# Parking the residual in DRAM during a mixture-of-experts stage, with half of one expert's up weights in its place

## The chip, the cores and the metric

The kernel runs on one core of one Trainium2 chip. The metric is device time in microseconds (us) of one execution; smaller is better.

## What is computed

One decoder layer for 256 prompt tokens and 8 sample tokens, 264 in all, in float32 with a model width of 1024. The part around the change is the second half:

```python
x = x + gate_m * jnp.einsum('ntd,de->nte', merged, lw['w_out'])
h2 = rmsnorm(x, lw['g_norm_ffn']) * (1.0 + scale_f) + shift_f
x = x + gate_f * moe_ffn(h2, lw)
...
a = jnp.einsum('td,edf->tef', hb, lw['w_e_gate'])
b = jnp.einsum('td,edf->tef', hb, lw['w_e_up'])
routed = jnp.einsum('tef,efd->td', jax.nn.silu(a) * b * gates[..., None], lw['w_e_down'])
```

There are 64 experts of inner width 256. Each has 2 MB of gate and up weights (called *up weights* here; 1 MB for each half of the 1024 input rows) and 1 MB of down weights. Each token goes to 8 experts. A shared expert is added to all tokens.

## The kernel before

Activations lie with features on the 128 partitions: `xT` is the residual (128 x 8 x 264), `hT` the normalised tokens. The first half of the program (attention, convolution and gate mixers, output projection) ends with the residual after the mixers in `xT`; each of its 8 tiles adds one to the semaphore `x1`. The same step makes `xa`, the scaled input of the second norm. After that `xT` is not read until the end of the program, when the sum of the experts is scaled and added to it (`scaled`, 16 VectorE operations) and it is stored as output.

**The handover to the experts.** The normalised tokens are transposed to rows (`h2tok`) and stored to a DRAM table `h2rows` together with the gates `lg`, from which GpSimd gathers each expert's tokens by indirect DMA. `hT` itself is stored to `h2kept` (read again only in a fallback for overfull experts), because its place then takes weights.

**The expert stage** goes over 32 pairs of experts (`pair(p)`, experts 2p and 2p+1). For each pair TensorE does the up product of the two halves (`up`: 32 matmuls of 64 x 512 into bank pA, 16 for each half of the input rows), spreads the result of the pair before to its tokens (`spread_samples`, `spread`), transposes the activations (`act_tr`), and does the down product (`down`, banks pB and pC). GpSimd gathers the tokens of pair q into `xs` (`gather`), three pairs ahead of their use in the steady state; VectorE computes the indices (`index`), the gates' column (`gate_column`) and the activation.

**The order of the transfers** is written by hand in SyncE's program: one queue, in which each transfer waits for its semaphores and all behind it wait too. `refill(p)` reloads the ring for pair p + 2: each half of the up weights after pair p has released it (semaphore `gu`), the down weights after `dn`. A 2 MB transfer brings one half of the up weights of both experts (16 KB a partition). Parts of three experts (KEPT = 19, DOWN = 37, AGAIN = 43) are loaded early into tensors that have become free, and left out of the refills (`alone`).

GpSimd issues the gathers on a queue of its own. Before the first gather it waits for the stores of the gates (`d_tok`) and rows (`d_rows2`), and for `idx`. SyncE waits for the first gather (`d_x[0]`) before it overwrites `hT`. These are the lines of the handover that set the order:

```python
pool.wait_ge(d_tok, 16 * 2)
pool.wait_ge(d_rows2, 16 * 3)
...
sp.wait_ge(d_x[0], 16)
sp.dma_start(hTf[:, 0:1024], expert_up(KEPT, 1, 2, 4).rearrange("p k c -> p (k c)")).then_inc(d_kept, 16)
```

The first is at line 823, the last two at 677 and 678.

Of the kernel before, what the change touches and what calls it, by code (L numbers as in the profile page):

```python
# [9 lines left out]
F32 = mybir.dt.float32  # L10
# [4 lines left out]
P = 128  # L15
D = 1024
DT = D // P
NP_ = 256
NS = 8
NT = NP_ + NS  # L20
# [10 lines left out]
E = 64  # L31
# [68 lines left out]
MID = KEPT // 2  # L100
DOWN = 2 * MID + 19
AGAIN = DOWN + 6


PLACE = (0, 3, 2, 1)
# [3 lines left out]
HALF_K = DT // 2  # L109
# [3 lines left out]
def place(e):  # L113

    return ORDER[(e - 1) % NSLOT]
# [92 lines left out]
def build(nc, A, O):  # L208

    with ExitStack() as ctx:  # L210
# [8 lines left out]
        xT = sb("xT", [P, DT, NT])  # L219
# [51 lines left out]
        lg = sb("lg", [P, 3, E])  # L271
# [42 lines left out]
        xa = pT[:].rearrange("p t n -> p (t n)")[:, 0:DT * NB].rearrange("p (k c) -> p k c", k=DT)  # L314
        free_p = pT[:].rearrange("p t n -> p (t n)")[:, DT * NB:NTILE * NT]
        shifts = ksq[:, 1, 0:3 * NC].rearrange("p (x c) -> p x c", x=3)
        h2tok = [xs[:, 0, 0:D], xs[:, 1, 0:D], qTf[:, 0:D]]
# [25 lines left out]
        sact = qTf[:, D:D + FT * NT].rearrange("p (f t) -> p f t", f=FT)  # L343
        sactg = [abuf[:, 512:512 + NT], rstd[:]]
        zpf = zp[:].rearrange("p k t -> p (k t)")
        first_gu = [adx[:, k, :] for k in range(CT)] + [kTf[:, k * 512:(k + 1) * 512] for k in range(CT)]
        hTf, h2f = hT[:].rearrange("p k t -> p (k t)"), free_p[:, 0:3 * D]
        wrf, bsf = wrou[:].rearrange("p k e -> p (k e)"), bsp[:].rearrange("p k t -> p (k t)")
# [17 lines left out]
        def up_part(b):  # L366
            return part(b, GU_AT[b], DT, 2 * FE)
# [3 lines left out]
        def up_halves(b):  # L371
            pair_at = ringf[:, PAIR_AT[b]:PAIR_AT[b] + 4 * DT * FE]
            return pair_at.rearrange("p (h x c) -> p h x c", h=2, x=2)[:, :, SECOND[b]]

        def up_rows(b):
            at = [PAIR_AT[b] + (2 * (k // HALF_K) + SECOND[b]) * HALF_K * 2 * FE + k % HALF_K * 2 * FE for k in range(DT)]
            return [ringf[:, x:x + 2 * FE] for x in at]
# [41 lines left out]
        d_in = sem("small_inputs")  # L419
# [7 lines left out]
        d_first = sem("first_expert")  # L427
# [19 lines left out]
        d_tok = sem("gates_stored")  # L447
        d_rows2 = sem("h2_stored")
        d_x = [sem("tokens_gathered0"), sem("tokens_gathered1")]
        c_f = sem("vector_chain_dense")  # L450
        norms = nc.dram_tensor("head_norms", (2, H, NT), F32, kind="Internal").ap()
        h2kept = nc.dram_tensor("h2_kept", (P, DT, NT), F32, kind="Internal").ap()
        h2rows = nc.dram_tensor("h2_rows", (NT, D + E), F32, kind="Internal").ap()

# [8 lines left out]
        def _(sp):  # L463
# [143 lines left out]
            def expert_down(e):  # L607
                return A["w_e_dn"][e // 2][:, 1 - e % 2]
# [20 lines left out]
            def two(w, p):  # L629
                return A[w][p] if isinstance(p, int) else A[w][bass.ds(p, 1)].rearrange(  # L630
                    "o p h x k c -> (o p) h x k c" if w == "w_e_gu" else "o p x k c -> (o p) x k c")
# [4 lines left out]
            def down_load(b, p, x, to):  # L636
                sp.dma_start(down_part(b), two("w_e_dn", p)[:, 1 - x]).then_inc(wgd[to], 16)
# [4 lines left out]
            def half_load(q, h, b):  # L642
# [12 lines left out]
            reuse(3, "exp")  # L655
            half_load(1, 1, 3)
            down_load(3, 0, 1, 3)
            n = BASE["rout"]
            sp.wait_ge(full[n % 4], n // 4 + 1)
            sp.dma_start(wrf, expert_down(KEPT)[:, 1, 0:512]).then_inc(d_kept, 16)  # L660
            sp.wait_ge(s["h2s"], 1)
            sp.wait_ge(s["h2"], DT)
            sp.dma_start(h2kept, hT[:]).then_inc(d_kept, 16)
# [1 line left out]
            sp.wait_ge(full[n % 4], n // 4 + 1)  # L665
            sp.dma_start(pT[:].rearrange("p t n -> p (t n)")[:, 0:FT * D], expert_down(0).rearrange("p f c -> p (f c)")
                         ).then_inc(d_first, 16)
            for j, m in enumerate((P, P, NS)):
                sp.wait_ge(s["h2tok"], 2 * j + 2)
                sp.dma_start(h2rows[j * P:j * P + m, 0:D], h2tok[j][0:m]).then_inc(d_rows2, 16)  # L670
            sp.wait_ge(s["mask_gates"], 2)
            sp.dma_start(h2rows[0:NP_, D:D + E].rearrange("(j p) e -> p j e", p=P), lg[:, 0:2, :]).then_inc(d_tok, 16)
            sp.dma_start(h2rows[NP_:NT, D:D + E], lg[0:NS, 2, :]).then_inc(d_tok, 16)
            sp.wait_ge(d_kept, 16 * 7)
            n = BASE["shup1"]
            sp.wait_ge(full[n % 4], n // 4 + 1)
# [9 lines left out]
            def refill(p, i):  # L686
                q = p + 2
                at = q if i is None else i * 2 + q
                alone = i is None and 2 * q + 1 in (KEPT, AGAIN)
                for h, (b, _) in enumerate((ups(q), second_ups(q))):  # L690
                    n = 2 * p + 1 + h
                    sp.wait_ge(s["gu"], n if i is None else i * 4 + n)
                    if alone:
                        sp.dma_start(up_halves(0)[:, h], two("w_e_gu", at)[:, h, 0].rearrange("p k c -> p (k c)")
                                     ).then_inc(wgt[b], 16)
                    else:
                        sp.dma_start(up_pair[q % 2 == 1][:, h], two("w_e_gu", at)[:, h].rearrange("p x k c -> p (x k c)")
                                     ).then_inc(wgt[b], 16)
                sp.wait_ge(s["dn"], 2 * p + 2 if i is None else i * 4 + (2 * p + 2))
                if q % 2:  # L700
                    down_load(0, at, 0, 0)
                    if i is not None or 2 * q + 1 not in (KEPT, AGAIN):
                        down_load(1, at, 1, 1)
                elif i is None and 2 * q + 1 == DOWN:
                    down_load(2, at, 0, 2)
                else:
                    sp.dma_start(down_pair, two("w_e_dn", at).rearrange("p x k c -> p (x k c)")).then_inc(wgd[2], 16)

            for h in range(2):
                sp.wait_ge(s["gu"], h + 1)  # L710
                sp.dma_start(up_part(1).rearrange("p (h k) c -> p h (k c)", h=2)[:, h], expert_up(4 + h, 1).rearrange("p k c -> p (k c)")
                             ).then_inc(wgt[1], 16)
                sp.dma_start([adx[:].rearrange("p k c -> p (k c)"), kTf[:, 0:CT * 512]][h],
                             expert_up(AGAIN, h).rearrange("p k c -> p (k c)")).then_inc(d_first, 16)
# [16 lines left out]
            with sp.Fori(0, (NPAIR - 14 - MID - 1) // 2) as i:  # L731
                for p in (MID + 12, MID + 13):
                    refill(p, i)
            refill(NPAIR - 3, None)

            sp.wait_ge(s["flag"], 1)
            over = sp.value_load(flag[0:1, 0:1], min_val=0, max_val=1)
# [111 lines left out]
        def _(pe):  # L849
# [82 lines left out]
            for m in range(6):  # L932
                n = BASE["in0"] + m
                t = enter(n)
# [40 lines left out]
            for h in range(H):  # L975
                n = BASE["q"] + h
                t = enter(n)
# [10 lines left out]
            for h2 in range(H // 2):  # L988
                n = BASE["k"] + h2
                t = enter(n)  # L990
# [6 lines left out]
            for b in range(2):  # L997
                n = BASE["v"] + b
                t = enter(n)
# [45 lines left out]
            t = enter(n)  # L1045
# [5 lines left out]
            t = enter(n)  # L1051
            for hf in range(2):
                for j in range(4):
                    h = 4 * hf + j
# [3 lines left out]
            m = BASE["qlatT"]  # L1058
            t = enter(m)
# [155 lines left out]
            for c in range(CT):  # L1215
                n = BASE["uvs"] + c
                t = enter(n)
# [62 lines left out]
            t = enter(n)  # L1280
# [117 lines left out]
            def up(p, i):  # L1398
                if p:
                    pe.wait_ge(s["xt"], turn(i, p + 1, 1))  # L1400
                else:
                    pe.wait_ge(s["h2x"], DT + 1)
                if 2 <= p < NPAIR - 2:
                    pe.wait_ge(s["idx"], turn(i, p + 3, 1))
                gu = []
                for e in (2 * p, 2 * p + 1):
                    if e == 0:
                        pe.wait_ge(d_first, 16 * 5)
                        gu.append(first_gu)
                    elif e == KEPT:  # L1410
                        pe.wait_ge(d_kept, 16 * 11)
                        gu.append(kept_gu)
                    elif e == AGAIN and i is None:
                        pe.wait_ge(d_first, 16 * 9)
                        gu.append(first_gu)
                    else:
                        if e == 1:
                            pe.wait_ge(wgt[1], arrival(1, "exp"))
                        elif e % 2 == 0:
                            b, n = ups(p)  # L1420
                            pe.wait_ge(wgt[b], turn(i, n, 8))
                        gu.append(up_rows(place(e)) if p else [up_part(place(e))[:, k, :] for k in range(DT)])
                for k in range(DT):
                    if k == HALF_K and p == 0:
                        pe.wait_ge(s["xt"], 1)
                    if k == HALF_K and p:
                        b, n = second_ups(p)
                        pe.wait_ge(wgt[b], turn(i, n, 8))
                    for x in range(2):
                        last = mm(pA[CAP * x:CAP * (x + 1), :], xTs[:, p % 2, k, CAP * x:CAP * (x + 1)], gu[x][k],  # L1430
                                  k == 0, k == DT - 1)
                    if k == HALF_K - 1:
                        last.then_inc(s["gu"], 1)
                last.then_inc(s["gu"], 1)
# [506 lines left out]
        def _(dve):  # L1941
# [624 lines left out]
            V.tensor_copy(gm_last, gm[(NPAIR - 1) % 4][:, 0:NT])  # L2566
            for p in range(29, NPAIR):
                pair(p)
            for m in range(DT):
                if m % 4 == 0:  # L2570
                    dve.wait_ge(s["spread"], 2 + m // 4)
                scaled(m, acc[m]).then_inc(s["sums"], 1)
# [168 lines left out]
```

## Time and profile before

| | us |
|---|---|
| median of 3 runs | 971.5 |
| lowest and highest run | 970.04, 972.77 |
| the profiled execution, its own time | 971.65 |
| span of the profiled execution | 969.8 |
| PE busy | 940.4 (97%) |
| DVE busy | 561.1 (58%) |
| ACT busy | 201.9 (21%) |
| DMA, mean over the span | 322 GB/s |

Granted TensorE clock: 0.997 over the span. Busy PE contains matmuls that are in flight and wait for their weights' turn, so 97% doesn't say that PE sets the time. Which engine does so differs from stage to stage; it is read from who waits for whom in a stretch, and from the rate of the DMA engines there. In the rows below, a time in the first column is us from the span's start, SPq is SyncE's queue of issued transfers, L860 is the helper that issues every matmul, and `oaT`, `qT`, `vtok` and `sinT` are tensors whose space the expert stage uses again (its activations, its transposed tokens, the pair's result, and small tables). `h_rows` is `h2rows`, `h_kept` is `h2kept`.

### The profile page before, as it was taken

What the parts mean: (1) busy time and instruction counts of PE and PEld (TensorE: products, weight loads), DVE (VectorE), ACT (ScalarE), POOL (GpSimd) and SP (SyncE); (2) the same over time, 40 slices, a digit from 0 to 9 for tenths busy, and PEclk for the clock granted to TensorE, in tenths of its full rate; (3) what the DMA queues carried; (4) which work ended last, traced back from release to release, by engine and by line L of the source; (5) the groups of instructions that cost most, each with busy time, mean ns of one, the idle gap of its engine ahead of it and who ended that gap; (6) DMA issues with size and microseconds to landing.
All of it is one profiled execution on the core that took longest, in us unless ns stands there. A gap on an engine that the chain in (4) does not pass through costs nothing.

```text
span 969.8 us, 15335 instructions
## 1 busy us (share of the span) xinstructions
PE 940.4 (97%) x5400; PEld 537.9 (55%) x5401; DVE 561.1 (58%) x1389; ACT 201.9 (21%) x416; POOL 56.3 (6%) x77
## 2 busy tenths in 40 slices
PE   6999999999999999999999999999999999999997
PEld 2488867544446788888644444444444344434343
DVE  2613322367864010123738877888888788886864
ACT  3321241335435200002511111111111111111111
POOL 0000010100000000000011000000100000000000
PEclk9999999999999999999999999999999999999999
DMA  8995559756546295537679999999999999999994
GB/s 304 419 416 237 183 193 324 229 155 171 169 136 271 99 384 222 217 130 282 263 299 424 424 425 424 396 423 423 429 424 425 423 424 422 426 427 423 422 428 156
DMA packets 54228, 312.03 MB, mean 322 GB/s; under 512 B 9018, under 2 KB 28506, under 8 KB 33426
## 3 DMA queue, kind: packets, MB, share of 16 engines
q1 hardware_dynamic: 47986, 298.10, 77.4%
q0 software_dynamic: 5904, 12.79, 3.7%
q8 instruction: 42, 0.69, 0.3%
q10 hardware_dynamic: 272, 0.26, 0.1%
q14 instruction: 24, 0.20, 0.1%
HBM read 315.80 MB, written 3.95 MB: 330 GB/s over the span
## 4 chain that ended last, share of the span: by engine, by line
PE 72%; DMA 19%; SPq 4%; DVE 2%; issue 2%; ACT 0%; DVEq 0%; POOLq 0%
PE bank L860 45%; PE pA L860 17%; DMA ring<-in_w_e_gu 16%; PE pB L860 4%; PE pC L860 4%; SPq L493 2%; PE pD L860 1%; DMA ring<-in_w_bg 1%; SPq L537 1%; DMA pT<-in_poolT 1%; PE pA L1439 0%; DMA xs<-h_rows,idx 0%; DVE rstd L1963 0%; DVE xT L2506 0%; SPq L532 0%
## 5 line engine op out<-in xcount | busy, mean ns | idle before, releaser
L860 PE MATMUL pA<-ring,qT 128*64 128x512 f32 x976 | 227.6, 594 | 9.2 <-DMA ring<-in_w_e_gu 9.2
L2489 DVE STREAM_TRANSPOSE qT<-xs 32x256 f32<-32x256 f32 x480 | 209.2, 436 | 7.7
L860 PE MATMUL bank<-hT,ring 128*128 128x264 f32 (+1 forms) x832 | 189.4, 388 | 0.9 <-DMA ring<-in_w_bg 0.9
L860 PEld LDWEIGHTS bank<-hT,ring 128*128 128x128 f32 (+1 forms) x832 | 154.3, 189 | 31.6 <-issue 4.7
L860 PEld LDWEIGHTS pA<-ring,qT 128*64 128x64 f32 x976 | 72.8, 137 | 154.0 <-issue 137.9
L860 PE MATMUL bank<-wuk,ring 128*128 128x512 f32 x192 | 87.0, 601 | 0.0
L860 PE MATMUL bank<-pT 128*128 128x256 bf16 (+1 forms) x499 | 85.4, 273 | 0.2 <-issue 0.2
L860 PE MATMUL bank<-pT,vtok 128*128 128x256 bf16 (+1 forms) x264 | 71.8, 281 | 0.0
L860 PE MATMUL pB<-ring,oaT 128*64 128x512 f32 x240 | 62.0, 605 | 0.0
L860 PE MATMUL pC<-ring,oaT 128*64 128x512 f32 x240 | 60.4, 592 | 0.0
L832 POOL DMA_INDIRECT xs<-h_rows,idx x32 | 36.0, 1125 | 407.1 <-DVE idx L2466 306.6
L860 PEld LDWEIGHTS bank<-wuk,ring 128*128 128x128 f32 x192 | 35.4, 192 | 41.9 <-issue 40.6
L2527 DVE SCALAR_TENSOR_TENSOR oaT<-oaT,sinT,pA 128x256 f32<-128x256 f32 x32 | 15.4, 480 | 74.3 <-ACT oaT L1902 74.3
L1902 ACT ACTIVATE oaT<-pA 128x256 f32<-128x256 f32 x32 | 12.3, 384 | 215.1 <-PE pA L860 215.1
L860 PEld LDWEIGHTS bank<-pT 128*128 128x128 bf16 x500 | 48.9, 98 | 6.3 <-issue 0.8
L2499 DVE TENSOR_TENSOR pT<-vtok 128x512 f32<-128x512 f32 x62 | 41.8, 686 | 12.2 <-ACT vtok L1912 10.0
L860 PE MATMUL bank<-pT,ring 128*128 128x264 f32 (+1 forms) x208 | 48.6, 388 | 0.0
L2082 DVE TENSOR_REDUCE xs<-ksq 128x8 f32<-128x512 f32 x48 | 32.3, 685 | 21.1 <-ACT ksq L1725 19.3
L860 PEld LDWEIGHTS bank<-pT,ring 128*128 128x128 f32 x208 | 39.3, 190 | 7.3 <-issue 0.4
L2503 DVE TENSOR_TENSOR pT<-pT 128x512 f32<-128x512 f32 x62 | 39.9, 684 | 0.0
L1912 ACT ACTIVATE vtok<-pB 128x512 f32<-128x512 f32 x32 | 19.1, 597 | 99.4 <-PE pB L860 99.4
L860 PEld LDWEIGHTS pC<-ring,oaT 128*64 128x64 f32 x240 | 18.4, 137 | 35.3 <-issue 35.3
(380 smaller groups left out, 914.6 us busy)
## 6 DMA issues: line engine op xcount, KB each, us to landing
ring<-in_w_e_gu SPq DMA_DIRECT2D x58, 2048.0 KB, 19.7
ring<-in_w_e_dn SPq DMA_DIRECT2D x34, 1024.0 KB, 16.2
ring<-in_w_e_dn SPq DMA_DIRECT2D x13, 2048.0 KB, 17.5
ring<-in_poolT SPq DMA_DIRECT2D x64, 208.0 KB, 2.8
ring<-in_w_ada SPq DMA_DIRECT2D x12, 1024.0 KB, 10.4
ring<-in_w_bg SPq DMA_DIRECT2D x4, 3072.0 KB, 11.0
ring<-in_w_mix SPq DMA_DIRECT2D x5, 2048.0 KB, 9.8
ring<-in_w_ada SPq DMA_DIRECT2D x4, 2048.0 KB, 12.9
```

The source lines that it names most:

```text
L493: return sp.value_load(ptab[0:1, bass.ds(x, 1)], min_val=0, max_val=NPOOL - 1)
L537: sp.dma_start(rowpg[g][x], A["poolR"][bass.ds(page(g * HALF + x), 1)] .rearrange("o r c -> (o r) c")).then_inc(d_rows, 16)
L832: nc.gpsimd.indirect_dma_start(out=xs[:, q % 2, :], out_offset=None, in_=h2rows, in_offset=bass.IndirectOffsetOnAxis(ap=idx[:, q % 2:q % 2 ...
L860: return nc.tensor.matmul(out, lhsT, rhs, start=start, stop=stop)
L1902: nc.scalar.activation(silu_s, pA[:, 0:FE], ACT.Silu).then_inc(s["silu_s"], 1)
L1912: nc.scalar.activation(yrow[:, hf * 512:(hf + 1) * 512], t[:], ACT.Copy).then_inc(s["y"], 1)
L2082: V.tensor_reduce(out=kss[:, q, j, :], in_=ksq[:, j % 2, :].rearrange("p (h d) -> p h d", h=H), op=ALU.add, axis=AX.X).then_inc(s["ksq_use ...
L2489: last = V.transpose(xTs[32 * j:32 * j + 32, q % 2, :, 32 * a:32 * a + 32], src[32 * a:32 * a + 32, j])
L2499: V.tensor_tensor(rest_y[:, c], yrow[:, c], parts_y[0][:, c], ALU.subtract).then_inc(s["rest"], 1)
L2503: V.tensor_tensor(low_y[:, c], rest_y[:, c], parts_y[1][:, c], ALU.subtract).then_inc(s["low"], 1)
L2527: V.scalar_tensor_tensor(out=act_s, in0=silu_s, scalar=gcol[:, p % 2:p % 2 + 1], in1=pA[:, FE:2 * FE], op0=ALU.mult, op1=ALU.mult).then_in ...
```

## The change

The residual is written to a new DRAM tensor `x1kept` as soon as its 8 tiles are there, and read back into `xT` by a transfer behind the last weights; VectorE waits for that before the final scaling. In between, `xT` holds the first half of the up weights of expert AHEAD = 41, and the refill of that half (pair 20, in `refill(18)`) brings only expert 40's: 1 MB where it was 2. In the handover the stores of token rows and gates stand ahead of the store of `hT` and of the load of expert 0's down weights. A wait for that load (`d_first`) is added ahead of the later loads that use its semaphore.

```diff
+AHEAD = AGAIN - 2
...
+        x1kept = nc.dram_tensor("x1_kept", (P, DT, NT), F32, kind="Internal").ap()
...
             half_load(1, 1, 3)
             down_load(3, 0, 1, 3)
+            sp.wait_ge(s["x1"], DT)
+            sp.dma_start(x1kept, xT[:]).then_inc(d_in, 16)
...
             sp.dma_start(wrf, expert_down(KEPT)[:, 1, 0:512]).then_inc(d_kept, 16)
+            for j, m in enumerate((P, P, NS)):
+                sp.wait_ge(s["h2tok"], 2 * j + 2)
+                sp.dma_start(h2rows[j * P:j * P + m, 0:D], h2tok[j][0:m]).then_inc(d_rows2, 16)
+            sp.wait_ge(s["mask_gates"], 2)
+            sp.dma_start(h2rows[0:NP_, D:D + E].rearrange("(j p) e -> p j e", p=P), lg[:, 0:2, :]).then_inc(d_tok, 16)
+            sp.dma_start(h2rows[NP_:NT, D:D + E], lg[0:NS, 2, :]).then_inc(d_tok, 16)
             sp.wait_ge(s["h2s"], 1)
             sp.wait_ge(s["h2"], DT)
             sp.dma_start(h2kept, hT[:]).then_inc(d_kept, 16)
...
-            for j, m in enumerate((P, P, NS)):
-                sp.wait_ge(s["h2tok"], 2 * j + 2)
-                sp.dma_start(h2rows[j * P:j * P + m, 0:D], h2tok[j][0:m]).then_inc(d_rows2, 16)
-            sp.wait_ge(s["mask_gates"], 2)
-            sp.dma_start(h2rows[0:NP_, D:D + E].rearrange("(j p) e -> p j e", p=P), lg[:, 0:2, :]).then_inc(d_tok, 16)
-            sp.dma_start(h2rows[NP_:NT, D:D + E], lg[0:NS, 2, :]).then_inc(d_tok, 16)
+            sp.wait_ge(d_in, 16 * 3)
+            sp.wait_ge(s["sq2"], DT)
+            sp.wait_ge(s["xa"], DT)
+            sp.dma_start(xTf[:, 0:2048], expert_up(AHEAD, 0).rearrange("p k c -> p (k c)")).then_inc(d_in, 16)
...
-                    if alone:
-                        sp.dma_start(up_halves(0)[:, h], two("w_e_gu", at)[:, h, 0].rearrange("p k c -> p (k c)")
+                    if alone or i is None and h == 0 and 2 * q + 1 == AHEAD:
+                        sp.dma_start(up_halves(0 if q % 2 else 2)[:, h], two("w_e_gu", at)[:, h, 0].rearrange("p k c -> p (k c)")
...
+            sp.wait_ge(d_first, 16 * 6)
...
             refill(NPAIR - 3, None)
+            sp.wait_ge(d_in, 16 * 4)
+            sp.dma_start(xT[:], x1kept).then_inc(d_in, 16)
...
+                        if e == AHEAD and i is None:
+                            pe.wait_ge(d_in, 16 * 4)
+                            gu[-1] = [xTf[:, k * 512:(k + 1) * 512] for k in range(HALF_K)] + gu[-1][HALF_K:]
...
             for p in range(29, NPAIR):
                 pair(p)
+            dve.wait_ge(d_in, 16 * 5)
```

SyncE's queue in the handover, before (`wrou` takes a part of KEPT's down weights, `pT` expert 0's down weights, `hT`, `ksq` and `abuf` parts of KEPT and DOWN):

```order
L637 DMA ring<-in_w_e_dn 128x2048
L660 DMA wrou<-in_w_e_dn 128x512
L663 DMA h_kept<-hT 128x2112
L666 DMA pT<-in_w_e_dn 128x2048
L670 DMA h_rows<-xs 128x1024 x2
L670 DMA h_rows<-qT 8x1024
L672 DMA h_rows<-lg 128x2x64
L673 DMA h_rows<-lg 8x64
L678 DMA hT<-in_w_e_gu 128x1024
L679 DMA hT<-in_w_e_dn 128x1024
```

And of the change (`x_kept` is `x1kept`):

```order
L640 DMA ring<-in_w_e_dn 128x2048
L662 DMA x_kept<-xT 128x2112
L665 DMA wrou<-in_w_e_dn 128x512
L668 DMA h_rows<-xs 128x1024 x2
L668 DMA h_rows<-qT 8x1024
L670 DMA h_rows<-lg 128x2x64
L671 DMA h_rows<-lg 8x64
L674 DMA h_kept<-hT 128x2112
L677 DMA pT<-in_w_e_dn 128x2048
L682 DMA xT<-in_w_e_gu 128x2048
L687 DMA hT<-in_w_e_gu 128x1024
L688 DMA hT<-in_w_e_dn 128x1024
```

The five stores of rows and gates have moved past two transfers of 1 MB, a store of the residual stands ahead of them, and three transfers of 1 MB now stand between them and the loads into `hT`.

SyncE's queue at the refills of pairs 20 to 22, of the change; before, the first of these rows and the second were one, of 128x4096 x2:

```order
L703 DMA ring<-in_w_e_gu 128x2048
L706 DMA ring<-in_w_e_gu 128x4096
L716 DMA ring<-in_w_e_dn 128x4096
L703 DMA ring<-in_w_e_gu 128x2048 x2
L640 DMA ring<-in_w_e_dn 128x2048
```

One transfer has half its width; nothing else has moved there.

## Rows read from the trace of the kernel before

**Rows 1.** GB/s of the DMA engines in 40 slices of the span, from the page.

```profile
GB/s 304 419 416 237 183 193 324 229 155 171 169 136 271 99 384 222 217 130 282 263 299 424 424 425 424 396 423 423 429 424 425 423 424 422 426 427 423 422 428 156
```

**Rows 2.** Waits in 494:732 (first row, TensorE's longest), then in 732:970.

```profile
PE pB L860 <- ACT oaT L1909: 0.7, 1, 0.7
...
PE pA L860 <- DMA ring<-in_w_e_gu: 9.2, 11, 1.3
```

**Rows 3.** Windows: us, PE, PEld, DVE, ACT, POOL busy, clock, DMA share, GB/s.

```profile
475.00:480.00 5.00, 5.00 (x29) 4.18 (x28) 4.53 (x46) 1.19 (x3) 0.00 (x0) 1.00 0.74 262
...
486.00:490.00 4.00, 4.00 (x21) 3.32 (x20) 2.87 (x14) 0.39 (x1) 1.49 (x2) 1.00 0.03 5
...
512.00:612.00 100.00, 100.00 (x633) 46.78 (x631) 79.80 (x199) 13.13 (x27) 6.97 (x7) 1.00 1.01 424
628.00:636.00 8.00, 8.00 (x55) 3.13 (x51) 5.78 (x14) 0.62 (x2) 0.57 (x1) 1.00 0.94 362
636.00:956.00 320.00, 310.76 (x1920) 135.96 (x1918) 252.59 (x619) 43.53 (x89) 21.65 (x20) 1.00 1.00 419
```

**Rows 4.** The chain of waits from the stores to the first expert: start, us, what.

```profile
483.85 2.86 DMA h_rows<-lg
...
488.00 4.07 DMA xs<-h_rows,idx
...
492.11 0.67 PE pB L1395 x4
```

**Rows 5.** Timeline: first row stores, index, last shared matmuls, second gather, pair 0.

```profile
480.24 1.30 SPq L670 DMA_DIRECT2D h_rows<-xs  x2
...
486.04 0.15 DVE L2466 TENSOR_SCALAR idx<-idxf 128x1 uint32<-128x1 f32 x1
...
488.65 3.06 PE L860 MATMUL bank<-hT,ring 128*128 128x264 f32 x13
...
489.76 0.99 POOL L832 DMA_INDIRECT xs<-h_rows,idx  x1 [0.51 <-issue]
...
493.95 0.60 SPq L643 DMA_DIRECT2D ring<-in_w_e_gu  x1
...
501.36 0.48 DVE L2527 SCALAR_TENSOR_TENSOR oaT<-oaT,sinT,pA 128x256 f32<-128x256 f32 x1 [5.76 <-ACT oaT L1902]
```

**Rows 6.** Transfers issued near 488, 489.8, 495.8 and 612.5: KB, us to landing.

```profile
xs<-h_rows,idx POOLq DMA_INDIRECT x1, 4.1
...
xs<-h_rows,idx POOLq DMA_INDIRECT x1, 3.5
...
xs<-h_rows,idx POOLq DMA_INDIRECT x1, 10.4
...
ring<-in_w_e_dn SPq DMA_DIRECT2D x1, 1024.0 KB, 6.8
xs<-h_rows,idx POOLq DMA_INDIRECT x1, 7.2
```

**Rows 7.** Transfers issued near 465.9, 475.4, 782.3, 493.9: KB, us to landing.

```profile
ring<-in_w_e_dn SPq DMA_DIRECT2D x1, 1024.0 KB, 10.5
...
h_kept<-hT SPq DMA_DIRECT2D x1, 1056.0 KB, 4.2
...
ring<-in_w_e_dn SPq DMA_DIRECT2D x1, 1024.0 KB, 17.2
...
ring<-in_w_e_gu SPq DMA_DIRECT2D x1, 2048.0 KB, 11.7
```

**Rows 8.** The end: chain, then the last two down loads, issued at 930.60.

```profile
923.61 26.58 DMA ring<-in_w_e_gu
...
950.23 3.65 PE pA L860 x16
...
961.86 0.48 DVE xT L2506
...
ring<-in_w_e_dn SPq DMA_DIRECT2D x2, 1024.0 KB, 23.1
```

More of the change, by code:

```diff
@@ L345, in build @@
         zpf = zp[:].rearrange("p k t -> p (k t)")
+        xTf = xT[:].rearrange("p k t -> p (k t)")
         first_gu = [adx[:, k, :] for k in range(CT)] + [kTf[:, k * 512:(k + 1) * 512] for k in range(CT)]
```

## The prediction

> **What bounds the kernel now.** I read the rate by slices first. From slice 21 (about 509 us) to slice 38 the DMA engines move 422 to 429 GB/s, but for one slice of 396 [rows 1]: the expert stage streams at a constant rate. Then who waits: between 494 and 732 us TensorE waits for no weights, its longest wait being 0.7 us for ScalarE; from 732 to the end its matmuls wait 9.2 us, in 11 waits, for up weights [rows 2]. So TensorE sets the pace at first, and from 732 us on the stream does. The chain at the end agrees: the last half of up weights lands at 950.2, and only then come the last 3.65 us of up matmuls [rows 8].
>
> What ties the two together is the last moment at which the stream had nothing to do. That is in 628:636, at 362 GB/s [rows 3]: 8 us x (424 - 362) / 424 = 1.2 us idle, because the refills of pair 9 are small and TensorE had not yet released the next slot. After it the stream has no gap (419 GB/s in 636:956, [rows 3]). So the end is: the time at which TensorE reaches that release, plus all bytes issued later over the rate. A byte less after 636 us shortens the kernel; whatever makes TensorE start the experts later by X lengthens it by X.
>
> That start is the handover. The chain there [rows 4]: the last gates' store is issued at 483.85 and lands 2.86 us later (486.71), GpSimd starts 1.3 us later, and the gather takes 4.07 us from 488.00 and lands at 492.07, TensorE goes on at 492.11. It had its last shared matmuls until 488.65 + 3.06 = 491.71 [rows 5], so it waited 0.4 us. The DMA engines stand nearly idle in 486:490, at 5 GB/s [rows 3].
>
> **The change part by part.**
>
> *Half of an expert less in the stream.* 1024 KB is 1.049 MB; at 424 GB/s [rows 3] that is 2.47 us. It is taken out of a refill issued near 757 us, when the stream is behind, so all of it counts if no new gap opens. The shortest time to landing in the expert stage after that is 17.2 us, for 1 MB issued near 782 [rows 7], a transfer that needs 2.5 us itself: some 12 us of queue are in front of it, and taking 2.5 away leaves it full. And TensorE must be able to use it: it has waited 9.2 us in this part [rows 2]. **-2.5 us.**
>
> *Store of the residual* (1056 KB). It is issued at about 466.7, behind 3 MB of loads of which the last lands at 465.9 + 10.5 = 476.4 [rows 7]. Its own 2.5 us then move the small load behind it and fill part of 475:480, which runs at 262 GB/s with room for 5 x 162 / 424 = 1.9 us [rows 3]. The store lands near 479, before the token rows are ready (their first store goes at 480.24, [rows 5]), and before SyncE's new wait for it. **0**; at worst, if it reaches into the rows' stores, +0.5.
>
> *Reading it back.* It is issued behind the last down loads. These land at 930.6 + 23.1 = 953.7 in the median of the two, about 955 for the second; the residual's 2.5 us end near 957.5, and VectorE's first scaling is at 961.86 [rows 8]. **0**, hidden by some 4 us; without that cover, what it is late.
>
> *New waits.* SyncE comes to those for `x1`, `sq2`, `xa` and the stored residual after their events, and to the one for the sixth `d_first` transfer (expert 0's down load) behind the first gather's landing, when that load is in. **0.** The store of `hT` and that down load are now issued behind the row stores, from 484.6. The first is needed by the load into `hT`, which waits for the gather anyway; the second by pair 0's down product, which comes after the activation at 501.36 [rows 5]. **0**; if either landed late, what it is late.
>
> *Stores of rows and gates first.* They are now issued as soon as VectorE and ScalarE have made the data, and still will be: moving them saves no issue time, only the transfer of expert 0's down weights in front of them. The last store took 2.86 us to land. It can gain at most what lies behind the index: `idx` is ready at 486.04 + 0.15 = 486.19 [rows 5], the stores land at 486.71, so 0.5 us. **-0.5 us** on the gather's start (0 to -0.5), which would be about 487.5. In quiet it would then land at 491.6, and TensorE, free at 491.7, would gain 0.4.
>
> *But the gather is no longer in quiet.* Behind the stores SyncE now issues `hT`'s store (1056 KB), expert 0's down weights (1024 KB) and the half expert (1024 KB), from about 484.6. Counting 1.7 us from issue to first byte (the `hT` store took 4.2 us to land, of which 2.5 are its bytes, [rows 7]), they occupy the engines from 486.3 to 493.8. The gather's own data moves from about 489.6. Now the gather has those 4 us to itself. What company costs it: in quiet 4.1 and 3.5 us; 7.2 beside one load of 1024 KB (rows of 8 KB, as here); 10.4 beside a load of 2048 KB (rows of 16 KB) [rows 6]. The 7.2 landed just after that load (6.8, issued within 0.3 us of it), and the 10.4 (495.8 + 10.4 = 506.2) just after the 2 MB load issued at 493.95, which took 11.7 [rows 5, 7]. So a gather shares each engine row by row with loads and needs about as long as its 8 rows' worth of them. The bounds: 0 (the gather isn't held up), and 4.2 us, the end of the backlog (493.8 - 489.6). The nearest row gives 7.2 - 3.8 = 3.4; one load of eight 8 KB rows an engine is worth 2.5. I take 2.5, since part of the 3.4 was another load of 16 KB rows in front. The gather then lands at 494.1 instead of 492.07: **+2.0 us** (-0.4 to +3.6) on TensorE's start, with nothing to absorb it.
>
> Sum against the profiled execution: 971.65 - 2.5 + 2.0 = 971.2; the median of the runs is 0.15 lower: **971.0 us**, -0.5 us. A measurement of this kernel can tell about 0.3% (2.9 us) from no change.
>
> On the sharing of an engine, the Trainium skill ("DMA: Bandwidth & Descriptors", section on queues, rings and completion order) has a rule: each DMA engine takes turns between queues by whole packets of some 9 to 17 descriptors, not row by row. By that rule the gather would wait only for the load in progress, and the sum would be lower, as rival 2 works out. The trace doesn't quite agree: the 7.2 us gather landed 0.4 us after a whole load issued behind it.
>
> **The rivals.**
>
> 1. *The gather isn't delayed.* For it: a gather has 128 slots and on average 264 x 8 / 32 = 66 tokens, so there is little to move, and GpSimd's queue is another one. Against: of the gathers in [rows 6], none beside a load took less than 7.2. Then TensorE starts 0.4 us earlier: 971.5 - 2.5 - 0.4 = **968.6**.
>
> 2. *It waits only for the transfer in progress.* At 489.6 that is expert 0's down load, whose data ends at about 486.3 + 5.0 = 491.3: 1.7 us of delay, landing at 493.3, X = +1.2: **970.2**.
>
> 3. *It waits for the whole backlog.* X = +3.6: 971.5 - 2.5 + 3.6 = **972.6**, slower, but by less than can be told.
>
> 4. *Slower than before: the second gather takes over the path.* It is issued at 489.76 [rows 5] on the same queue, behind the first, and VectorE waits for it (`gate_column(1)`) ahead of pair 0's activation, which runs at 501.36 [rows 5]. Before, it took 3.5 us and was early by 8. If its rows are not served before the 2 MB load that SyncE issues after the first gather lands (now 493.95, landing at 505.6, [rows 5, 7]), it lands with that load: 4.3 us after the activation needs it, and with rival 3's X the sum is 971.5 - 2.5 + 3.6 + 4.3 = **976.9**. It decides from the point at which the second gather lands later than about 503. Against: between the backlog's end and that load stand four small loads of 1.5 MB, room enough to get through.
>
> 5. *The change doesn't do what it says*: nothing is gained if TensorE, not the stream, sets the last third. The time would be 971.5 + 2.0 = 973.5. But it waited 9.2 us for weights there [rows 2], more than three times what is taken away: excluded.
>
> **How the numbers follow.** Forecast 0.50; rival 1 0.20; rival 2 0.12; rival 3 0.10; rival 4 0.06; anything else 0.02. The likeliest case gives 971.0. The range takes in rival 1 below and rival 3 above, with 0.3 for the measurement: 968.3 to 973.0; rival 4 is left out. Rival 1 lies right at the bound of 0.3%: half of it, and a little for a second gain that I don't see, make faster 0.15; rival 4 and the rest make slower 0.07; same 0.78.
>
> **What the profile would show.** The refill of pair 20 with one row of 1024 KB; from then on, landings 2.5 us earlier relative to TensorE's first expert matmul. The first gather issued at about 487.5 and landing 6 to 7 us later, with the DMA engines over 400 GB/s in 487:494. TensorE waiting some 2.4 us for `xs` before its transposes, where it waited 0.4. The idle 1.2 us of the stream still there, moved by X. The residual's read landed before VectorE asks. I am wrong if the first gather lands within 5 us of its issue, or if the last up weights don't land X - 2.5 us from where they did, or if VectorE waits for the second gather.

## The result, and the profile after

| | before | changed |
|---|---|---|
| median of 16 runs each | 971.54 us | 974.10 us |
| ratio, 95% interval | | 1.0025 (1.0017 to 1.0033) |
| the profiled execution, span | 969.8 us | 971.7 us |

The kernel became 2.6 us slower. That is under the 0.3% that I called the bound, but clear of the noise, on the other side than the forecast of -0.5, and outside the range (968.3 to 973.0). One execution of the changed kernel took 5593 us; it is in the median and not in the ratio.

The two profiled executions differ before the handover already: the index is ready at 486.04 in one and at 484.49 in the other, though nothing ahead of it is known to cost more or less. Two profiles of one and the same kernel (load behind gather, below) differ as much: they have it at 484.42 and 487.37. So the handover is measured from the start of the index computation, not from zero. The chain of waits of the changed kernel there, in the columns start, us and what, beside [rows 4, 5]:

```profile
484.49 0.16 DVE idx L2481
...
484.88 1.13 issue
486.01 7.76 DMA xs<-h_rows,idx
...
493.81 0.67 PE pB L1407 x4
...
495.56 8.35 PE pA L872 x32
```

The gather takes 7.76 us where it took 4.07. From the index to the first expert matmul it was 493.74 - 486.04 = 7.70 us; it is 495.56 - 484.49 = 11.07, so **+3.4**. Then comes what I had not in the sum: pair 0's up product, 32 matmuls, takes 8.35 us, where the same chain before has 7.02 us for it, **+1.3**. Windows of the changed kernel (columns as in [rows 3]) show why:

```profile
486.00:490.00 4.00, 4.00 (x20) 3.13 (x18) 2.01 (x9) 0.39 (x1) 2.24 (x2) 1.00 0.98 394
490.00:494.00 4.00, 0.35 (x3) 0.19 (x3) 0.99 (x3) 0.00 (x0) 0.38 (x1) 1.00 0.70 280
494.00:496.00 2.00, 1.75 (x11) 1.06 (x12) 0.62 (x2) 1.08 (x2) 0.00 (x0) 0.70 0.51 115
496.00:498.00 2.00, 2.00 (x6) 0.47 (x4) 1.33 (x8) 0.00 (x0) 0.37 (x1) 0.50 0.99 394
498.00:500.00 2.00, 2.00 (x12) 0.74 (x10) 0.00 (x0) 0.00 (x0) 0.65 (x1) 0.95 1.15 420
```

The DMA engines, idle in 486:490 before, now move 394 GB/s. TensorE, with nothing to do from 490.2 to 493.8, is granted half its clock (0.50, that is 1.2 GHz instead of 2.4) in 496:498, and three pairs of matmuls take 0.86 us a step instead of 0.43. The clock fell only after the wait: it is 1.00 in 494.0:494.5, where the transposes run, and 0.50 from 495.0 on. The last two transfers that stand in SyncE's queue ahead of the gather, by their own landings (KB, us from issue to landing):

```profile
pT<-in_w_e_dn SPq DMA_DIRECT2D x1, 1024.0 KB, 7.1
xT<-in_w_e_gu SPq DMA_DIRECT2D x1, 1024.0 KB, 10.3
```

The first, issued at 482.71, lands at 489.8, the second, issued at 483.25, at 493.6, and the gather at 493.77: 0.2 us after the last byte that was queued ahead of it.

At the end, chain, then VectorE's timeline, then TensorE's waits in 732:970 of the changed kernel:

```profile
925.49 26.58 DMA ring<-in_w_e_gu
...
952.11 3.65 PE pA L872 x16
```

```profile
959.48 3.23 DVE L2521 SCALAR_TENSOR_TENSOR xT<-bank,ada,xT 128x256 f32<-128x256 f32 x8 [2.71 <-DMA xT<-x_kept]
...
963.74 0.48 DVE L2521 SCALAR_TENSOR_TENSOR xT<-bank,ada,xT 128x256 f32<-128x256 f32 x1 [0.90 <-PE bank L872]
```

```profile
PE pA L872 <- DMA ring<-in_w_e_gu: 8.2, 10, 1.2
```

The end is still the stream's [rows 8]. From the end of pair 0's up product (500.76 before, 503.91 now) to the last up weights it takes 448.2 us, where it took 449.5: 1.3 less, of the 2.5 expected. TensorE's waits for up weights in 732:970 are 8.2 us where they were 9.2 [rows 2]. The ten profiles of kernels that load the half expert, this one among them, gain between 0.6 and 2.5 us in this stretch, the three of kernels without it (below) between -0.2 and +0.15; what sets the size within that spread is not shown. The residual's read lands late enough to hold VectorE 2.7 us, but the wait is covered: from the last up weights to VectorE's ninth scaling it is 11.63 us before and after.

### The profile page after: what moved, and what is told of

It reads as the page before. It is cut to its first block, busy times and chain, and to the rows that moved or that the text cites. A ratio compares the mean times of both kernels' runs of the same rounds, so it can differ in the third digit from the quotient of the medians.

```text
span 971.7 us, 15342 instructions
## 1 busy us (share of the span) xinstructions
PE 940.5 (97%) x5400; PEld 538.4 (55%) x5401; DVE 561.4 (58%) x1389; ACT 201.8 (21%) x416; POOL 56.3 (6%) x77
## 4 chain that ended last, share of the span: by engine, by line
PE 73%; DMA 17%; SPq 6%; issue 2%; DVE 2%; ACT 0%; DVEq 0%; POOLq 0%
PE bank L872 44%; PE pA L872 18%; DMA ring<-in_w_e_gu 13%; PE pB L872 5%; PE pC L872 4%; SPq L496 3%; PE pD L872 1%; SPq L540 1%; DMA ring<-in_w_bg 1%; SPq L535 1%; DMA pT<-in_poolT 1%; DMA xs<-h_rows,idx 1%; PE pA L1454 0%; DVE xT L2521 0%; DMA ring<-in_poolT 0%
## 5 line engine op out<-in xcount | busy, mean ns | idle before, releaser
L872 PE MATMUL bank<-wuk,pT 128*128 128x512 f32 x64 | 30.9, 634 | 7.7 <-DMA pT<-in_poolT 7.7
```

Of the source, the lines that this page charges most:

```text
L872: return nc.tensor.matmul(out, lhsT, rhs, start=start, stop=stop)
```

## The experiments

Each is a short edit of one of the two kernels; the kernel before ran beside them. "Handover" is the time from the index to the first expert matmul, less the 7.70 us of before, plus the up product of pair 0 less 7.02, both from one profiled execution each. "Time" is the median less that of the kernel before on the same chip. The kernels are named by what they do; "rows first" means that the rows and gates are stored ahead of `hT`.

| kernel | residual parked | half expert's load | rows first | handover, us | time, us | ratio, 95% |
|---|---|---|---|---|---|---|
| changed | yes | ahead of gather | yes | 3.4 + 1.3 | +2.6 | 1.0017 to 1.0033 |
| order alone | no | none | yes | 0.1 + 0 | -0.2 | 0.9985 to 1.0010 |
| parking, old order | yes | none | no | 3.0 + 0.5 | +3.7 | 1.0027 to 1.0048 |
| parking, new order | yes | none | yes | -0.1 + 0 | -1.2 | 0.9983 to 1.0004 |
| all, old order | yes | ahead of gather | no | 2.5 + 1.5 | +1.0 | 0.9997 to 1.0024 |
| load behind gather | yes | behind it | yes | 0.1 + 0 | **-2.1** | 0.9966 to 0.9989 |
| the same again | | | | 0.1 + 0 | **-1.8** | 0.9974 to 0.9993 |
| store behind gates | yes, later | behind it | no | 0.4 + 0 | -1.4 | 0.9972 to 0.9994 |
| load ahead of rows | yes | first | yes | 1.9 + 0 | +0.6 | 1.0001 to 1.0023 |
| load behind landing | yes | ahead, held | no | 3.4 + 1.7 | +3.3 | 1.0013 to 1.0034 |
| warm | as changed | | | 4.2 + 0 | +1.2 | 0.9995 to 1.0024 |
| one more store | as changed | | | 5.8 + 2.0 | +5.5 (one run) | |
| two more stores | as changed | | | 5.8 + 0.5 | +6.6 (one run) | |

**All, old order.** The changed kernel with the stores of the rows and gates back behind `hT`'s store and expert 0's down load, ahead of the half expert's load.

```diff
-            for j, m in enumerate((P, P, NS)):
-                sp.wait_ge(s["h2tok"], 2 * j + 2)
-                sp.dma_start(h2rows[j * P:j * P + m, 0:D], h2tok[j][0:m]).then_inc(d_rows2, 16)
-            sp.wait_ge(s["mask_gates"], 2)
...
-            sp.dma_start(h2rows[NP_:NT, D:D + E], lg[0:NS, 2, :]).then_inc(d_tok, 16)
...
+            for j, m in enumerate((P, P, NS)):
+                sp.wait_ge(s["h2tok"], 2 * j + 2)
+                sp.dma_start(h2rows[j * P:j * P + m, 0:D], h2tok[j][0:m]).then_inc(d_rows2, 16)
+            sp.wait_ge(s["mask_gates"], 2)
...
+            sp.dma_start(h2rows[NP_:NT, D:D + E], lg[0:NS, 2, :]).then_inc(d_tok, 16)
```

> The changed kernel with the old order of the stores: hT's store and expert 0's down load ahead of the rows and gates, and the half expert's load directly behind the gates. Theory A (the change loses only in the handover: the first gather lands with the last transfer queued ahead of it, and TensorE, having waited, starts at half its clock): now only 1 MB is queued behind the gates and its data is through before the gather's own begins, so the gather takes 4 to 5 us again, TensorE waits under 1 us, its clock stays at 1.0, and the 2.5 us in the stream are kept: 1.5 to 2.5 us faster than the kernel before, about 969.3. Rival B (parking the residual itself costs: its store, its reading back, or the added waits): still as slow as the changed kernel, ratio 1.001 to 1.003 to the kernel before. Rival C (the 2.5 us of the stream are not there to be had): time equal to the kernel before.

Not faster: +1.0 us. The gates themselves are late in it:

```profile
483.48 5.58 DMA h_rows<-lg
...
490.35 4.17 DMA xs<-h_rows,idx
...
496.31 8.53 PE pA L872 x32
```

The gather is quiet again (4.17 us), as theory A had it, but the last store of the gates takes 5.6 us to land instead of 2.9 [rows 4], TensorE waits 2.8 us, and the clock falls. So something ahead of the gates or behind them is new, and this kernel cannot say which.

**Order alone.** The kernel before, with the same six lines moved the other way: ahead of `hT`'s store and expert 0's down load, and the wait for `d_first` that goes with it. Nothing is parked and no load added.

```diff
+            for j, m in enumerate((P, P, NS)):
+                sp.wait_ge(s["h2tok"], 2 * j + 2)
+                sp.dma_start(h2rows[j * P:j * P + m, 0:D], h2tok[j][0:m]).then_inc(d_rows2, 16)
+            sp.wait_ge(s["mask_gates"], 2)
...
+            sp.dma_start(h2rows[NP_:NT, D:D + E], lg[0:NS, 2, :]).then_inc(d_tok, 16)
...
-            for j, m in enumerate((P, P, NS)):
...
-            sp.dma_start(h2rows[NP_:NT, D:D + E], lg[0:NS, 2, :]).then_inc(d_tok, 16)
```

> The kernel before with the new order alone: rows and gates stored ahead of hT's store and expert 0's down load, no parking and no half expert. Theory A: 2 MB are now queued between the gates and the gather and end some 2 to 2.5 us sooner than the 3 MB of the changed kernel; the gather takes 5.5 to 6.5 us, TensorE waits 1 to 2 us, and with nothing won in the stream the time is 0.5 to 3 us above the kernel before, the more if the wait is long enough to halve the clock. If the new order itself were a gain (gates 0.5 us sooner), the time would be 0.4 us below.

```profile
486.58 4.58 DMA xs<-h_rows,idx
...
pT<-in_w_e_dn SPq DMA_DIRECT2D x1, 1024.0 KB, 7.0
```

Neither loss nor gain. With 2 MB behind the gates the gather takes 4.6 us, half a microsecond more than in quiet, given back by the gates' earlier landing. The expected 5.5 to 6.5 us was wrong. The second of the two transfers, issued at 483.28, is not through when the gather is issued; it lands at 490.3, 0.9 us ahead of it. One transfer still in progress, with nothing behind it, costs half a microsecond. It is the third megabyte, queued behind that one, that does the harm.

**Load behind gather.** The changed kernel, with the half expert's load and its waits moved behind the last load ahead of the refills.

```diff
-            sp.dma_start(xTf[:, 0:2048], expert_up(AHEAD, 0).rearrange("p k c -> p (k c)")).then_inc(d_in, 16)
...
             half_load(2, 0, 2)
+            sp.dma_start(xTf[:, 0:2048], expert_up(AHEAD, 0).rearrange("p k c -> p (k c)")).then_inc(d_in, 16)
```

> The changed kernel with the half expert's load moved behind the wait for the gather (behind the first 2 MB load of pair 2). Theory A: the gather meets the same 2 MB as in the order-alone kernel and takes 5.5 to 6.5 us; the stream gets 1 MB more early, where it has 1.2 to 1.7 us of slack before pair 9, and 1 MB less later: about 1 us gained, so 0 to 2 us above the kernel before, and under the changed kernel by 1 to 2 us. Rival B (parking costs): no better than the changed kernel.

```profile
485.94 4.59 DMA xs<-h_rows,idx
...
492.21 7.02 PE pA L872 x32
```

-2.1 us, better than expected, and better than both kernels. From the end of pair 0's up product to the last up weights it takes 2.1 us less than before. The early stream takes the megabyte into the gap that it had: the window 628:636, which ran at 362 GB/s [rows 3], is now nearly full.

```profile
628.00:636.00 8.00, 8.00 (x61) 4.10 (x58) 6.02 (x16) 0.77 (x2) 0.00 (x0) 1.00 0.99 414
```

**Warm.** The changed kernel, with sixteen matmuls that compute nothing used, ahead of the wait for the gather.

```diff
             shared_up("shup1", FE + P, range(DT))
+            pe.wait_ge(s["h2tok"], 6)
+            for _ in range(16):
+                mm(pC[:, 0:P], ones[:], ones[:], True, True)
             tokens_tr(0)
```

> The changed kernel with 16 matmuls of 128x128 on ones (3.4 us of work whose result isn't used) in TensorE's program where it waits for the gather. Theory A's second half: the granted clock stays at 1.0, pair 0's up product takes 7.0 us instead of 8.4, and the time is 1.3 us below the changed kernel, about +0.9 us to the kernel before. Rival: the slow first matmuls come from something else (DMA traffic on the weights' memory, the transposed tokens late), and the time stays at the changed kernel's, +2.4 us.

The gather takes 8.7 us, and yet pair 0 runs at full clock: windows of this kernel, the granted clock third from the end.

```profile
494.00:496.00 2.00, 0.98 (x9) 0.79 (x8) 0.42 (x2) 0.00 (x0) 0.00 (x0) 1.00 0.05 13
496.00:498.00 2.00, 1.75 (x12) 0.82 (x12) 0.77 (x2) 1.08 (x2) 0.00 (x0) 1.00 0.66 176
```

The up product is back at 7.02 us with the same queue, so the 1.3 us were the clock's and not the traffic's. The time is at +1.2, 1.4 under the changed kernel's, near the 1.3 expected, but the two intervals overlap, and the 1.4 is not the clock alone: in the profiles this kernel's handover is 0.8 us longer before the first matmul, and from the end of the up product to the last up weights it takes 951.14 - 504.17 = 447.0 us, 2.5 less than before, where the changed kernel took 1.3 less.

**One more store.** The changed kernel, with `hT` stored once more, to a place that nobody reads. SyncE waits for that store before it loads over `hT`, so the time of this kernel and of the one with two holds more than the gather's delay.

```diff
             sp.dma_start(xTf[:, 0:2048], expert_up(AHEAD, 0).rearrange("p k c -> p (k c)")).then_inc(d_in, 16)
+            sp.dma_start(h2more, hT[:]).then_inc(d_in, 16)
```

> The changed kernel with one more store of hT (1056 KB, to a tensor that nothing reads) behind the half expert's load and ahead of the gather. Theory A (a gather lands only when everything queued ahead of it is through): the gather takes about 2.5 us longer than in the changed kernel, 10 to 11 us. Rival (the gather takes turns row by row with the load it meets, so it is through with its eight rows' worth of company): it stays at 7.8 to 8.7 us.

The gather takes 9.7 us, between the two theories; two more stores, below, tell them apart.

**Parking, old order.** The kernel before, with the residual stored, its place left empty and read back late, and the waits of the change.

```diff
+            sp.wait_ge(s["x1"], DT)
+            sp.dma_start(x1kept, xT[:]).then_inc(d_in, 16)
...
+            sp.dma_start(xT[:], x1kept).then_inc(d_in, 16)
...
+            dve.wait_ge(d_in, 16 * 4)
```

> The kernel before with the parking alone: the residual stored and read back, nothing loaded in its place, stores in the old order, all refills whole. Theory A: no cost, within 0.5 us of the kernel before. Rival B (parking costs): 1 us or more above it.

+3.7 us, where theory A had no cost. The chain, then the landings of `hT`'s store and of expert 0's down load:

```profile
482.74 5.72 DMA h_rows<-lg
...
489.75 4.14 DMA xs<-h_rows,idx
...
493.94 1.11 PE pB L1404 x4
```

```profile
h_kept<-hT SPq DMA_DIRECT2D x1, 1056.0 KB, 7.2
...
pT<-in_w_e_dn SPq DMA_DIRECT2D x1, 1024.0 KB, 7.3
```

Before, they landed in 4.2 us [rows 7] and 4.9. The residual's store, 1 MB earlier in the same queue, pushes each transfer behind it back by 2.4 to 3 us, down to the gates, which land in 5.7 us instead of 2.9. TensorE waits 2.9 us (491.05 to 493.94), and here the clock is at 0.50 before it resumes: its transposes take 1.11 us instead of 0.67. This also explains the all-old-order kernel, whose gates took 5.6.

**Load ahead of rows.** The changed kernel, with the half expert's load and its waits moved up, behind KEPT's small load.

```diff
             sp.dma_start(wrf, expert_down(KEPT)[:, 1, 0:512]).then_inc(d_kept, 16)
+            sp.dma_start(xTf[:, 0:2048], expert_up(AHEAD, 0).rearrange("p k c -> p (k c)")).then_inc(d_in, 16)
...
-            sp.dma_start(xTf[:, 0:2048], expert_up(AHEAD, 0).rearrange("p k c -> p (k c)")).then_inc(d_in, 16)
```

> The changed kernel with the half expert's load ahead of the rows' stores, as soon as the residual's store has landed, where the DMA engines stand idle for some 2 us. Its bytes are through some 2.5 us before the gather's begin, but the rows and gates are now stored behind it. If small stores land late only because of what is queued AHEAD of them: gates land about 1 us later than the index is ready, the gather takes 4.6 us as in the order-alone kernel, and the time is 1 to 2.5 us below the kernel before. If, as the run with the old order suggests, the gates' stores are also held up by the loads queued BEHIND them (there the last store, 2 KB, took 5.6 us against 2.9), they now land only with hT's store or expert 0's down load, 2 to 3 us after the index, and the time is 0 to 2 us above the kernel before.

+0.6 us, in the second branch. The gather starts 487.82 - 484.70 = 3.1 us after the index began, where order alone has 1.5, and takes 4.8 us. What stands ahead of the rows' stores is enough to explain it; whether loads behind small stores delay them too, these kernels don't separate.

**Load behind landing.** The all-old-order kernel, where the half expert's load waits until the rows and gates have landed.

```diff
+            sp.wait_ge(d_tok, 16 * 2)
+            sp.wait_ge(d_rows2, 16 * 3)
             sp.dma_start(xTf[:, 0:2048], expert_up(AHEAD, 0).rearrange("p k c -> p (k c)")).then_inc(d_in, 16)
```

> The old order of stores with the half expert's load held until the rows' and gates' stores have landed. If in the old-order run the load held up the stores queued in front of it, the stores now land in 2.9 us and the gather starts as in the kernel before, 1.8 us after the index. Its data then meets one load of 1 MB with 1 to 1.5 us still to go: 4.5 to 6 us instead of 4.1. TensorE waits 1 to 2 us; time 0.5 to 2 us below the kernel before, against +1.0 for the old-order run.

```profile
484.12 6.00 DMA h_rows<-lg
...
491.42 4.80 DMA xs<-h_rows,idx
```

Missed: +3.3 us. Its gates take 6.0 us with nothing behind them, so the load behind was not to blame. The load then starts only at 490.1 and meets the gather, which takes 4.8 us beside it and lands 0.6 us after it.

**Store behind gates.** The load-behind-gather kernel, with the stores of the rows and gates in the old order and the residual's store behind them.

```diff
-            sp.dma_start(x1kept, xT[:]).then_inc(d_in, 16)
             sp.dma_start(wrf, expert_down(KEPT)[:, 1, 0:512]).then_inc(d_kept, 16)
...
             sp.dma_start(h2rows[NP_:NT, D:D + E], lg[0:NS, 2, :]).then_inc(d_tok, 16)
+            sp.dma_start(x1kept, xT[:]).then_inc(d_in, 16)
```

> Old order of the stores, with the residual's store moved behind the gates' and the half expert's load behind the gather. If the parking cost 3.7 us only because its store stood ahead of hT's and pushed everything up to the gates back, that is gone: the gates' last store lands in about 2.9 us again, the store's own bytes go through the idle 486 to 489 us, the gather takes 4 to 5 us, and the time is that of the kernel with the load behind the gather, 1.5 to 2.5 us below the kernel before. If the parking costs in another place (the end, the early stream), it stays 1 us or more above.

```profile
484.23 3.25 DMA h_rows<-lg
...
488.78 4.16 DMA xs<-h_rows,idx
```

-1.4 us, just short of the 1.5 to 2.5 expected. The parking's cost is gone without the new order, by putting its store into the idle stretch. The gather takes 4.2 us although the window 486:490 is busy to 301 GB/s, for the store is through (landing at 490.0) when its rows come.

**Two more stores.** The kernel with one more store, with a second one behind it.

```diff
+            sp.dma_start(h2most, hT[:]).then_inc(d_in, 16)
```

> The kernel with one more store of hT, and a second one behind it: 5.3 MB queued between the gates and the gather instead of 4.3 and 3.2. If a gather had to wait for all that is queued ahead of it, 2.5 us more than with one, 12 us or more. If it takes turns with what it meets, no more than with one: 9 to 10.5 us, as the gathers do in the full stream of the expert stage.

```profile
h_more<-hT SPq DMA_DIRECT2D x1, 1056.0 KB, 13.3
h_most<-hT SPq DMA_DIRECT2D x1, 1056.0 KB, 14.7
xT<-in_w_e_gu SPq DMA_DIRECT2D x1, 1024.0 KB, 10.8
xs<-h_rows,idx POOLq DMA_INDIRECT x1, 9.7
```

9.7 us again, landing at 498.4, ahead of both added stores (near 500 and 502.7), though both were issued before it. So a gather doesn't wait for all that is queued ahead of it: with one added store and with two it is delayed by the same 5.6 us. That it takes turns with what it meets is the reading that fits; then, with one megabyte left to meet, turns and waiting for the end come to the same, as in the changed kernel. The Trainium skill ("DMA: Bandwidth & Descriptors", section on queues, rings and completion order) says that an engine takes turns between queues; this run fits that. That a gather waits only for the load in progress, as I read the rule for rival 2, doesn't hold in the changed kernel: 7.8 us.

**The same again.** 

> The kernel with the half expert's load behind the gather once more, to see whether its gain holds: 1.3 to 2.9 us below the kernel before.

-1.8 us: the gain holds.

**Parking, new order.** The parking's edit on the order-alone kernel.

> Parking alone, in the new order of the stores: the fourth of the four cases with the order alone (-0.2 us to the kernel before), the parking alone in the old order (+3.7) and the kernel before. Theory A (the parking costs only by what its store pushes back in the handover, and the new order takes the rows and gates out of that queue): within 0.5 us of the kernel before; the stream's gain is then the difference of this to the kernel with the load behind the gather, 1.5 to 2.5 us. Rival B (the parking costs elsewhere too): 1 us or more above.

-1.2 us by the medians, -0.6 by the ratio (0.9994), with an interval that reaches to +0.04%, so not told from no change. The forecast was within 0.5 us: both lie just outside it, on the side of a gain, and neither is clear of it. In the profile its handover is that of the kernel before. The parking costs nothing once the rows and gates stand ahead of `hT`'s store. The difference to the load-behind-gather kernel, which is the half expert's gain alone, is 0.7 to 1.0 us in medians and 1.9 in the profiles (last up weights 456.3 us after the first expert matmul here, 454.4 there); 1.5 to 2.5 was expected. The medians come from different chips and don't place the gain better than that.

## Why the prediction was wrong

- **The step that failed is "But the gather is no longer in quiet"**, twice over. Its size: I took +2.0 us within -0.4 to +3.6, by "one load of eight 8 KB rows"; the handover gave +3.4 for it, at the upper end, where rival 3 stood (the gather landed 0.2 us after the whole backlog, though the two more stores show that this is no rule). I had the nearest row, 3.4 us of company beside one 1 MB load [rows 6], and talked it down to 2.5. Those 7.2 us were also misread beside the page's rule: issued at 612.53 and 612.80, gather and load landed 0.1 us apart, not 0.4.
- Its consequence: "with nothing to absorb it" was right, but something multiplied it. TensorE's wait of 3.7 us cost another 1.3 us at half clock. No term, bound or rival of the sum held that; the warm kernel, with the same traffic and the clock kept up, does the product in 7.02 us. With 3.4 and 1.3 in it, the sum would have been -2.5 + 4.7 = +2.2, against +2.6 measured. The closeness owes something to chance: in the profile the stream gave 1.3, so that the last up weights come 3.4 us later after the index (X - 2.5 would be 2.2), and the two spans differ by 1.9 only because the index itself was 1.55 us earlier.
- **The stream's -2.5 us** was right in kind and at the upper end in size: 1.3 in the changed kernel, 2.5 in the warm one, 2.1 twice where the load takes the early gap. Why the changed kernel got half of it stays open.
- **"Store of the residual: 0"** was right for this kernel by luck of its other part. I priced its own landing, not what it does to the queue behind it: alone, in the old order, the parking costs 3.7 us. I looked for a cost at the token rows and gates, which the new order had taken out of its way, and so missed what the new order is there to save: not 0.5 us, but all of that 3.7.
- **The read back** was hidden, but by a misread row. VectorE's scalings begin at 955.79 before, not at 961.86, which is the ninth:

```profile
955.79 3.23 DVE L2506 SCALAR_TENSOR_TENSOR xT<-bank,ada,xT 128x256 f32<-128x256 f32 x8 [0.90 <-PE bank L860]
```

The real cover in the changed kernel is 1.0 us (the eight end at about 962.7, the ninth starts at 963.74), not 4.
- Rival 4 (the second gather) did not come: issued at 488.21, it landed at 494.1, long before pair 0's activation. Rivals 1 and 2 are excluded by the 7.8 us.

## What to carry to other kernels

A transfer put into an idle stretch is free only if it is through before the next short, latency-bound transfer begins: here the same megabyte held the handover up by 4.7 us in front of a gather and by 0.1 behind it, and only behind it was the stream's gain of 2 us left. Price a moved or added transfer by what it does to each one behind it in the queue, down to the one on which another engine waits. And where an engine's wait grows by some microseconds, look whether the TensorE clock survives it; the loss comes on top.

## What the runs showed of the hardware

- A gather (66 rows on average) took 4.1 to 4.2 us where all that was queued ahead of it was through by 1.6 us after its issue, 4.4 to 4.8 where one transfer was then still in progress and landed 0.6 to 1.1 us before it, 7.8 and 8.7 with a whole 1 MB load behind the one in progress, 9.7 with a store of 1 MB behind that load, and also with two.
- The granted clock fell to 0.50 after waits of TensorE of 2.8, 2.9, 3.7, 3.8 and twice 5.6 us, and stayed at 1.00 after one of 2.3 (load ahead of rows). What it took from pair 0's up product ranged from 0.5 to 2.0 us; where it fell before TensorE resumed, the transposes paid too (1.11 us for four, instead of 0.67).
- The last store of the gates, 2 KB, landed 2.9 us after its issue in the kernel before and 5.6 to 6.0 us with one more megabyte ahead in the same queue.
- Two profiles of one kernel placed the same instruction in mid-kernel at 484.42 and 487.37 us, and the stretches behind it agreed to 0.1 us: compare stretches from a common event.
